# One-core hybrid mLSTM/GLA layer: the first projection's gate weights, the merging stage's first inputs and the last stores moved across stage boundaries

## The reference

```python
(q_m, k_m, v_m, o_m, gate_m, q_g, k_g, v_g, r_g, lr_g, mg_m, mg_g) = jnp.split(h @ w_in, cuts, axis=-1)
...
hm_f, st_mf = mlstm_scan(qm, km, vm, gm[0, 0], gm[0, 1], st_mf, with_output)
...
og_f, st_gf = gla_scan(qg, kg, vg, split_heads(log_a[0], GLA_HEADS), st_gf, with_output)
...
y_m = merge_heads_rms(hm_f + flip_t(hm_b), ml_norm, h.dtype) * jax.nn.sigmoid(o_m)
y_g = merge_heads_rms(og_f + flip_t(og_b), gla_norm, h.dtype) * jax.nn.silu(r_g)
y = jax.nn.sigmoid(mg_m) * (y_m @ w_proj_m) + jax.nn.sigmoid(mg_g) * (y_g @ w_proj_g)
return y @ w_out, states
```

## Time and profile before

| | |
|---|---|
| median of 3 runs | 2381.39 us (2381.06 to 2385.33) |
| profiled execution, its time | 2384.28 us |
| its span in the trace | 2382.6 us |
| busy: PE, DVE, ACT, POOL | 2151.0, 1409.5, 1026.5, 835.2 us |
| granted TensorE clock, mean | 0.95 of full |
| DMA | 399.28 MB, mean 168 GB/s |

### The profile page before, as it was taken

The page is one execution under the profiler, slowest core; times in us unless marked ns, Lnnn a source line. Parts: engine busy times, 40 slices in busy tenths (PEclk is TensorE's granted clock), DMA queues, the critical chain, the costliest instruction groups (busy, mean ns, idle before and its releaser), DMA issues. The chain is left out here.

```text
span 2382.6 us, 26535 instructions
## 1 busy us (share of the span) xinstructions
PE 2151.0 (90%) x10128; PEld 1737.7 (73%) x10128; DVE 1409.5 (59%) x1688; ACT 1026.5 (43%) x1352; POOL 835.2 (35%) x614
## 2 busy tenths in 40 slices
PE   7979999998898995999999679999779999999992
PEld 1268887886687884888888567787667787887881
DVE  1539541100333324888988346445488899998993
ACT  2322311111244445556555334533256666676762
POOL 5300000001356654566766321220123344444431
PEclk9989999999899996999999889999979999999996
DMA  8633315211754765344454475564379965559425
GB/s 313 227 89 94 112 53 203 80 49 51 249 177 155 186 163 195 103 123 123 131 141 124 109 232 186 176 231 146 120 271 381 361 182 159 153 174 350 116 47 168
DMA packets 266538, 399.28 MB, mean 168 GB/s; under 512 B 30566, under 2 KB 190438, under 8 KB 259628
## 3 DMA queue, kind: packets, MB, share of 16 engines
q1 hardware_dynamic: 236428, 240.24, 31.9%
q0 software_dynamic: 27968, 147.89, 19.9%
q10 hardware_dynamic: 2016, 9.45, 1.0%
HBM read 402.22 MB, written 88.67 MB: 206 GB/s over the span
## 5 line engine op out<-in xcount | busy, mean ns | idle before, releaser
L2883 DVE TENSOR_TENSOR ex_w_lo<-ex_raw,ex_w_hi 128x2048 fp32r<-128x2048 f32 x186 | 416.1, 2283 | 40.8 <-ACT ex_w_hi L2745 40.5
L2745 ACT ACTIVATE ex_w_hi<-ex_raw 128x2048 fp32r<-128x2048 f32 x182 | 337.5, 1909 | 180.2 <-DMA ex_raw<-in_w_up_dram,rt_w_rows 99.0
L851 POOL DMA_DIRECT2D vals<-rows_out x40 | 21.8, 545 | 438.7 <-ACT rows_out L843 438.7
L2615 POOL DMA_INDIRECT ex_raw<-in_w_up_dram,rt_w_rows x60 | 76.3, 1271 | 143.0 <-DVE ex_w_lo L2883 137.8
L2615 POOL DMA_INDIRECT ex_raw<-in_w_down_dram,rt_w_rows x30 | 49.9, 1662 | 184.7 <-DVE ex_w_lo L2883 159.4
L936 PE MATMUL gl_u_ps<-half_hi,gl_u_w_hi 128*128 128x512 f32 x256 | 108.4, 423 | 3.5 <-ACT gl_u_exp L954 3.5
L936 PE MATMUL ml_u_ps<-half_hi,ml_u_w_hi 128*128 128x512 f32 x256 | 105.7, 413 | 6.5 <-ACT ml_u_exp L954 6.5
L2360 PE MATMUL mo_ps<-mo_branch_hi,mo_w_hi 128*128 128x512 f32 x256 | 106.3, 415 | 4.4 <-DVE mo_w_lo L2197 3.5
L2674 PE MATMUL ex_g_ps<-ex_w_hi,ex_x_hi 128*128 128x512 f32 x248 | 103.3, 417 | 7.5 <-DVE ex_x_lo L2888 7.4
L843 ACT ACTIVATE rows_out<-rows_ps 128x512 f32<-128x512 f32 x40 | 23.9, 598 | 198.3 <-PE rows_ps L810 198.3
L2674 PE MATMUL ex_y_ps<-ex_w_hi,ex_hidden_hi 128*128 128x512 f32 x248 | 100.0, 403 | 7.1 <-DVE ex_w_lo L2883 7.1
(11 more groups left out here) (440 smaller groups left out, 6055.2 us busy)
## 6 DMA issues: line engine op xcount, KB each, us to landing
fr_w<-in_w_mod_dram SPq DMA_DIRECT2D x10, 2048.0 KB, 9.8
ml_u_w<-in_w_in_dram SPq DMA_DIRECT2D x32, 512.0 KB, 5.1
gl_u_w<-in_w_in_dram SPq DMA_DIRECT2D x32, 512.0 KB, 5.2
vals<-rows_out POOLq DMA_DIRECT2D x40, 256.0 KB, 2.3
ml_v<-vals SPq DMA_DIRECT2D x20, 512.0 KB, 4.2
gl_v<-vals SPq DMA_DIRECT2D x20, 512.0 KB, 3.4
qk_w<-in_w_in_dram SPq DMA_DIRECT2D x16, 512.0 KB, 5.0
ml_rows<-scan_rows SPq DMA_DIRECT2D x16, 512.0 KB, 5.8
```

What stands on the lines that cost most here:

```text
L2615: pool.indirect_dma_start(out=raw[:, q, :], out_offset=None, in_=sources[q], in_offset=bass.IndirectOffsetOnAxis(ap=w_rows[:, q, b:b + 1], ...
L2745: act.activation(hi[:, q, h], raw[:, q, h], ACT.Copy).then_inc(hi_done[q], 1)
L2883: dve.tensor_tensor(lo[:, q, at], raw[:, q, at], hi[:, q, at].bitcast(F32), ALU.subtract)\
```

## The change

Three places. In `front`, POOL clears a tile `qk_gate_w` behind the masks and SP issues the six narrow loads of tile 0 there, behind its last weight load; `project_qk` finds them loaded. At the end of `gla_scan`, SP loads the first two weight tiles of `mix_out` (`merge_w`), the four token tiles of round 0 and the first four gates (both into `early`, which is the scan's tile of level keys, free after its last level matmul); ScalarE squares tile 0 ahead of its last copy of the scan's output and tiles 1 to 3 at its end. The waits for the last gate stores and accumulating stores move from the end of `gla_scan` into SP's list in `mix_out`. There, `first_norms` starts from the squares, `gate_branch` takes gates 0 to 3 from `early`, and PE turns three blocks ahead of unit 0 and the other five between its matmuls.

```diff
@@ front, SP
+            def load_first_heads():
+                src = w["w_in"][0].rearrange("(k p) n -> p k n", p=P)
+                sp.wait_ge(m.qk_cleared, 1)
+                for at, col, n in m.gate_columns:
+                    sp.dma_start(m.qk_raw[:, :, at:at + n], src[:, :, col:col + n]).then_inc(m.qk_loaded, 16)
...
+                if n == NB - SLOTS:
+                    load_first_heads()
@@ front, POOL
             build_masks(m, pool, masks_built)
+            pool.memset(m.qk_raw[:, :, :], 0.0).then_inc(m.qk_cleared, 1)
@@ project_qk, SP and POOL
             load(1)
-            load(0)
-            sp.wait_ge(cleared, 2)
+            sp.wait_ge(cleared, 1)
...
-            pool.memset(raw[:, 0, :, :], 0.0).then_inc(cleared, 1)
+            pool.memset(bias[:, :], 0.0).then_inc(cleared, 1)
             pool.wait_ge(cleared, 1)
-            pool.memset(bias[:, :], 0.0).then_inc(cleared, 1)
-            pool.wait_ge(cleared, 2)
@@ gla_scan, SP
+            wsrc = w["w_proj_m"][0].rearrange("(k p) n -> p k n", p=P)
+            for j in range(2):
+                sp.dma_start(m.merge_w[:, j, :, :], wsrc[:, :, j * P:(j + 1) * P]).then_inc(m.merge_w_loaded[j], 16)
+            sp.wait_ge(lv_made, PAIRED * OUTS)
+            for t in range(NL // 2):
+                sp.dma_start(hm_tile(t), m.hm[t * P:(t + 1) * P, :]).then_inc(m.hm_loaded[t], 16)
+            for g in range(EARLY_GATES):
+                sp.dma_start(m.early_gate(g), m.gates[0, g * P:(g + 1) * P, 0:HALF]).then_inc(m.gate_loaded[g], 16)
             units.store(sp, UNITS - 2)
             units.store(sp, UNITS - 1)
-            units.all_stored(sp)
             for d in range(2):
                 sp.wait_ge(o_stored[d], 16 * FIRST_VISITS)
-                sp.wait_ge(o_added[d], 16 * (OUTS // 2 - FIRST_VISITS))
@@ gla_scan, ScalarE
+            def hm_squares(t):
+                act.wait_ge(m.hm_loaded[t], 16)
+                if t >= 2:
+                    act.wait_ge(hm_squared, HEADS * (t - 1))
+                for h in range(HEADS):
+                    junk = (l1p, z)[t % 2][:, h // 2, h % 2 * DV:(h % 2 + 1) * DV]
+                    act.activation(junk, hm_tile(t)[:, h * DV:(h + 1) * DV], ACT.Square,
+                                   accum_out=m.hm_squares[:, HEADS * t + h:HEADS * t + h + 1]).then_inc(hm_squared, 1)
             units.take(act, UNITS - 1)
+            act.wait_ge(b_ready, STEPS)
+            hm_squares(0)
             leave(STEPS - 1)
             units.finish(act, UNITS - 2)
             units.finish(act, UNITS - 1)
+            for t in range(1, NL // 2):
+                hm_squares(t)
@@ mix_out, SP
-            load_in(0)
-            for g in range(OG):
+            for g in range(EARLY_GATES, EARLY_GATES + OG):
                 load_og(g)
-            load_w(0)
-            load_w(1)
             sp.dma_start(spread[:, :, :], m.mod_rows[:, D:3 * D].rearrange("p (a n) -> p a n", a=2))\
                 .then_inc(const_loaded, 16)
+            for j in range(2):
+                sp.wait_ge(m.units_stored[j], 16 * (UNITS // 2))
+            load_mg(0)
+            load_w(2)
+            load_mg(1)
+            for d in range(2):
+                sp.wait_ge(m.o_added[d], 16 * (OUTS // 2 - FIRST_VISITS))
             sp.dma_start(h2[:, 0, :], w["g_norm2"][0:1, :].partition_broadcast(P)).then_inc(const_loaded, 16)
-            load_mg(0)
-            for g in range(KD):
+            for g in range(EARLY_GATES, KD):
                 load_og(g + OG)
-                if g == KD // 2 - 1:
-                    load_w(2)
-                    load_mg(1)
             load_in(1)
@@ mix_out, ScalarE
+            def first_norms(pair):
+                two = slice(2 * HEADS * pair, 2 * HEADS * (pair + 1))
+                act.activation(st[:, 0, 1, two], m.hm_squares[:, two], ACT.Ln, bias=m.eps[:, 0:1], scale=1.0 / DV)\
+                    .then_inc(first_log, 1)
+                act.wait_ge(first_log, pair + 1)
+                act.activation(st[:, 0, 2, two], st[:, 0, 1, two], ACT.Exp, scale=-0.5).then_inc(rstd, 1)
...
-            norms(0, 0)
-            norms(0, 1)
+            first_norms(0)
+            first_norms(1)
@@ mix_out, TensorE
-            for g in range(KD):
+            AHEAD = 3
+            for g in range(AHEAD):
                 turn(g)
             for u in range(LAST):
-                unit(u)
+                unit(u, {k: k + AHEAD for k in range(KD - AHEAD)} if u == 0 else {})
```

More of the change, by code:

```diff
@@ L431, in project_qk @@
         ps = [ctx.enter_context(nc.psum_tensor(f"qk_ps{j}", [P, 3 * 512], F32)) for j in range(2)]
-        w_loaded = [sem(f"qk_w_loaded{j}") for j in range(2)]
+        w_loaded = (m.qk_loaded, sem("qk_w_loaded1"))
         (cleared, bias_loaded, hi_done, lo_done, made, small_left, image, left_g, tap, conv, done) = (
@@ L570, in weight_hi @@
                     act.wait_ge(made, s - 1)
-                act.activation(w_hi[:, j, :, :], raw[:, j, :, :], ACT.Copy).then_inc(hi_done, 1)
+                act.activation(w_hi[:, j, :, :], raw[j][:, :, :], ACT.Copy).then_inc(hi_done, 1)
             def leave(s):
@@ L881, in visit_of_other, with __init__ @@
     return 2 * i + 1 - u % 2
+EARLY_GATES = 4
 class GateUnits:
     GATE_COLS = (OM, RG, MGM, MGG)
-    def __init__(self, nc, m, ctx, sem, w, tag, half):
+    def __init__(self, nc, m, ctx, sem, w, tag, half, out=None, stored=None):
         sb = lambda n, s, dt=F32: ctx.enter_context(nc.sbuf_tensor(f"{tag}_{n}", s, dt))
@@ L895, in __init__ @@
         self.e = sb("u_exp", [P, 2, HALF])
-        self.out = sb("u_out", [P, 2, HALF])
+        self.out = sb("u_out", [P, 2, HALF]) if out is None else out
         self.ps = ctx.enter_context(nc.psum_tensor(f"{tag}_u_ps", [P, HALF], F32))
-        self.w_loaded, self.stored = ([sem(f"{tag}_u_{n}{j}") for j in range(2)] for n in ("w_loaded", "stored"))
+        self.w_loaded = [sem(f"{tag}_u_w_loaded{j}") for j in range(2)]
+        self.stored = [sem(f"{tag}_u_stored{j}") for j in range(2)] if stored is None else stored
         (self.hi_done, self.lo_done, self.made, self.kept, self.left, self.plus, self.logged, self.gate,
@@ L1336, in gla_scan @@
         o_ps, st_ps = bank("gl_o_ps", 2), bank("gl_st_ps", 2)
-        units = GateUnits(nc, m, ctx, sem, w, "gl", 1)
-        v_loaded, k_loaded, q_loaded, o_stored, o_added = ([sem(f"gl_{n}{d}") for d in range(2)] for n in (
-            "v_loaded", "k_loaded", "q_loaded", "o_stored", "o_added"))
+        units = GateUnits(nc, m, ctx, sem, w, "gl", 1, out=m.late_units, stored=m.units_stored)
+        v_loaded, k_loaded, q_loaded, o_stored = ([sem(f"gl_{n}{d}") for d in range(2)] for n in (
+            "v_loaded", "k_loaded", "q_loaded", "o_stored"))
+        o_added = m.o_added
         q_exp = sem("gl_q_exp")
@@ L2182, in gate_branch @@
                 dve.wait_ge(turned, g + 1)
-                dve.wait_ge(og_loaded[g % OG], 16 * (g // OG) + 16)
+                if g < EARLY_GATES:
+                    dve.wait_ge(m.gate_loaded[g], 16)
+                    gate = m.early_gate(g)
+                else:
+                    dve.wait_ge(og_loaded[g % OG], 16 * ((g - EARLY_GATES) // OG) + 16)
+                    gate = og[:, g % OG, :]
                 if g >= 2:
@@ L2337, in turn, with unit @@
                 last.then_inc(turned, 1)
-            def unit(u):
+            def unit(u, between={}):
                 hf, q, b = where(u)
@@ L2362, in unit @@
                     last = pe.matmul(out, a_hi, b_lo_, start=False, stop=(k == KD - 1))
+                    if k in between:
+                        turn(between[k])
                 last.then_inc(made, 1)
@@ L3025, in build @@
         m.router_bias = place(top, "router_bias", [P, GROUPS + EXPERTS])
+        m.hm_squares = place(top, "hm_squares", [P, NL // 2 * HEADS])
+        m.hm_loaded = [nc.alloc_semaphore(f"hm_loaded{t}") for t in range(NL // 2)]
+        m.gate_loaded = [nc.alloc_semaphore(f"gate_loaded{g}") for g in range(EARLY_GATES)]
+        m.merge_w_loaded, m.units_stored, m.o_added = (
+            [nc.alloc_semaphore(f"{n}{j}") for j in range(2)] for n in ("merge_w_loaded", "units_stored", "o_added"))
+        tail = top.enter_context(ExitStack())
         with ExitStack() as gla:
@@ L3031, in build @@
             m.lr = place(gla, "lr", [96, 2, T], F32R)
+            m.rank_w = place(gla, "rank_w", [96, 2, HEADS * DK], F32R)
             m.half_hi = place(gla, "half_hi", [P, KD, HALF], F32R)
@@ L3050, in build @@
                     m.tokens = tokens
+                    gates = split.enter_context(ExitStack())
+                    m.qk_raw = place(gates, "qk_gate_w", [P, KD, P], side="right")
+                    m.qk_loaded, m.qk_cleared = sem("qk_w_loaded0"), sem("qk_w_cleared")
+                    m.gate_columns = [(0, GATE, 4), (16, LR, RANK), (32, GATE + 8, 4), (48, LR + RANK, RANK),
+                                      (64, GATE + 4, 4), (96, GATE + 12, 4)]
```

(6 more changed lines are left out.)

62 lines of the change are left out of this document (31 added, 31 removed).

## The result

The changed kernel took 2365.74 us (median of 4 runs, 2359.78 to 2368.35); the kernel before took 2381.51 beside it (4 runs, 2381.06 to 2385.33). The ratio is 0.9931, 95% interval 0.9916 to 0.9946: 15.8 us faster in the medians. Its own executions spread more than I had written at the start: 8.6 us here and 10.3 in the second timing, 0.4% and not 0.2%. The profiled execution took 2368.35 us with a span of 2366.3. Forecast were 2364.8 us and, for a profiled execution, 2367.7.

What follows compares the result with a forecast made beforehand. PE was busy for 90% of the span, so only its idle stretches or low-clock time could pay. 8.5 + 8.1 = 16.6 us off the median 2381.39 gave 2364.8 us (2367.7 for a profiled execution), range 2361 to 2370.5.

Steps and rivals of the forecast that it cites:

- The first boundary: Entry of `project_qk`: with the column loads moved into `front`, PE starts at 124.81 instead of 133.27, 8.46 us.
- the cover of 5.4 us: End of `front`: the moved loads cost nothing, being issued at least 5.4 us ahead of PE's last batch.
- The lower bound's slower remainder: Entry of `project_qk`: VectorE's remainder may take 1.65 us instead of 1.2 beside POOL's memsets, leaving 8.0 us.
- Nothing is won there: First stretch of `project_qk`: the clock is at its lower level (0.50) and will be again, so no gain.
- One sign of being wrong: In `front`: PE's last batch starting late, not at 110.4, would show the prediction wrong.
- The entry of the second boundary: From `gla_scan` to `mix_out`: SP's 4.1 us wait goes, squares are added, entry at 1360.83, 0.4 us later than before.
- The squares take the place of the wait: End of `gla_scan`: 12 squares, 4.81 us, behind ACT's last instruction replace SP's wait of 4.1 us.
- The start of `mix_out`: PE's first turn at 1367.2 instead of 1373.91; the eighth branch ends at 1381.6 instead of 1389.72, 8.1 us earlier.
- Unit 3 hangs on the eighth branch: In `mix_out`: unit 3's time depends on the end of the eighth `gate_branch`, not on PE; 1400.7 instead of 1408.78.
- The 19.06 us: In `mix_out`: time from the end of the eighth `gate_branch` to unit 3, taken to stay the same.
- New loads in the way: Rival: the new loads delay PE's batch in `front`, or PE stays cold; gain 9 to 14 us, about 2369; chance 0.13.
- Slower: Rival: unit 0's short bursts in `mix_out` keep the clock at 0.50 into the dense units; over 2381 us; chance 0.02.

Runs made afterwards that it cites:

- the second timing: The changed kernel timed once more, unchanged: ratio 0.9937 to the kernel before.
- experiment 1: The kernel before with only the first boundary changed (memset and six column loads in `front`): ratio 0.9959 to the kernel before.
- experiment 6: The changed kernel with the 16 squares back in `mix_out`, its tiles, gates and weights still loaded early: ratio 0.9963 to the kernel before.
- experiment 9: The kernel of experiment 6 with POOL's last accumulating store issued at the start of `mix_out`: ratio 0.9934 to the kernel before.
- experiment 4: The changed kernel with the waits for the last stores back at the end of `gla_scan`: ratio 0.9932 to the kernel before.
- experiment 8: The changed kernel with gates 6 and 7 loaded on entry to `mix_out`, into two unused tiles: ratio 0.9940 to the kernel before.
- experiment 5: The changed kernel with unit 3's weights issued ahead of the slow column loads in `mix_out`: ratio 0.9919 to the kernel before.

## Why the prediction was right

The time came out 0.9 us over the forecast for the median and 0.7 for the profiled execution. The terms fit worse than that, and part of the fit is luck, since single executions of the kernel lie up to 10 us apart. The spans of the two traces differ by 16.3 us: 6.6 up to the start of PE in `project_qk` (8.4, less 1.8 of the dip in `front`), 0.9 more to the last copy of the scan (0.6 of it the shorter time at the low clock), 7.9 at the second boundary and 0.8 behind unit 3, which no run explains.

**The first boundary, 8.5 us: right.** Shown by experiment 1 (9.8 us, interval 6.7 to 12.6) and by the start of PE, 2.39 us behind the entry instead of 10.83: 8.44. The loads in `front` cost nothing, as the cover of 5.4 us said: where the clock didn't dip, the entry came at 122.41 instead of 122.44. The lower bound's slower remainder didn't come. "Nothing is won there" at the low clock was wrong in size: it ended 1.3 us sooner behind PE's start, some 0.6 us of gain. One sign of being wrong did show, PE's last batch in `front` at 112.16 and not 110.4, but from the dip and not from the loads.

**The entry of the second boundary: 0.7 us off, the reason wrong.** Forecast was an entry 0.4 us later against the last copy, measured 1.1 us. "The squares take the place of the wait" was the step that failed. The squares ended as forecast, 8.1 us behind the start of the last copy against 8.2, and would have allowed the entry at 1351.24 + 1.62 = 1352.9. What came last was POOL's accumulating store, 7.6 us in flight, and by experiments 6 and 9 it holds the stage. Without the new loads it was 5.5 us in flight (experiment 1) and 5.6 (before), beside them 6.3 to 7.6 in nine traces. I had read SP's 4.1 us as the only thing behind ACT, and costed the removal of the wait as if it freed the entry. Under it lay the next bound: in experiment 1 that store landed at 1343.20 + 5.5 = 1348.7, 2.9 us ahead of the entry of 1351.59, so without SP's wait some 0.9 us could have been had, and no more. With the change, experiment 4 gives the moved waits 0.6.

**The start of `mix_out`: right.** First turn 6.2 us behind the entry (forecast 6.4), eighth branch over 20.9 behind it (20.8), unit 3 39.3 behind it (39.9), PE's wait ahead of it 3.4 (2 to 3). Experiment 6 prices the squares in the first of these: with them back in `mix_out` the first turn is 11.2 us behind the entry, 5.0 more. It isn't the whole 6.4, because there the first scaling runs beside the later squares.

**"Unit 3 hangs on the eighth branch": right for this change, not as a rule.** The 19.06 us became 18.4 here and 19.2 in experiment 8, where half of what the branch gained was lost again on the way.

**The rivals.** New loads in the way: the right place to look, with the wrong victim. They didn't slow PE's batch in `front`. What they stood beside was POOL's store, which made the entry 1.1 us later than the squares alone allowed; that the loads are what made it slow is argued from the flight times above. Slower: in the changed kernel the clock rose near 1370 us, within unit 0, and units 1 and 2 ran at 1.00. The swing that stands behind this rival (the Trainium skill, TensorE: Matmul & The Clock Gate, "A second HAM failure mode: psum-queue depth-cycling": with short pauses between groups of matmuls the clock swings between its two levels) is in these traces all the same. The kernel before had it around the start of unit 0, and experiment 5 at the border to unit 1. In the changed kernel the clock fell once more too, but behind one long wait, the 3.4 us for unit 3's weights. One stretch of each, in this order:

```profile
1382.00:1390.00 8.00, 5.69 (x17) 4.57 (x18) 3.19 (x5) 2.14 (x4) 3.61 (x4) 0.50 0.61 193
```

```profile
1374.00:1376.00 2.00, 2.00 (x5) 1.62 (x6) 1.54 (x2) 0.99 (x1) 0.00 (x0) 0.50 0.96 342
```

```profile
1394.00:1396.00 2.00, 2.00 (x6) 1.58 (x5) 0.00 (x0) 1.94 (x9) 0.00 (x0) 0.50 0.78 229
```

In the last two it was low for about 3 us of dense work (a matmul of 128x512 took 0.63 us instead of 0.40), a loss of some 1.5 us each, not of 12.

## What to carry to other kernels

Where a wait ends a stage, ask what lies right under it before it is counted as a gain: list everything still in flight at the boundary, the DMAs that GpSimd issued too, and take the second latest. Work moved under such a bound is free as long as it ends first, and pays where it came from, as the 16 squares did. When the bound is known, move it together with the work: here that brought the next stage's entry a further 3.6 us forward.
